# One layer with a chunked RWKV-7 recurrence: turning the triangular inverse with full transposes, and merging two state products

## The reference

```python
def step(s, inp):
    r_t, w_t, k_t, v_t, z_t, b_t = inp
    sz = jnp.einsum('bhvk,bhk->bhv', s, z_t)
    s = s * w_t[:, :, None, :] + sz[..., None] * b_t[:, :, None, :] + v_t[..., None] * k_t[:, :, None, :]
    return s, jnp.einsum('bhvk,bhk->bhv', s, r_t)
w = jnp.exp(-DECAY_SCALE * jax.nn.sigmoid(w0[d] + jnp.tanh(xw) @ w_lora[d]))
a = jax.nn.sigmoid(a0[d] + xa @ a_lora[d])
```

## Time and profile before

| | |
|---|---|
| median of 3 runs | 2143.8 us (2142.92 to 2143.82) |
| span of the profiled execution, first to last instruction | 2138.7 us |
| median less span | 5.1 us |
| TensorE busy, whole span | 2041.2 us (95%) |
| VectorE busy | 1196.4 us (56%) |
| ScalarE busy | 727.9 us (34%) |
| GpSimd busy | 234.2 us (11%) |
| recurrence, first X record to last | 594.5 to 863.4 us |

### The profile page before, as it was taken

One profiled execution on the slowest core, in us unless ns is written; L12 is line 12 of the kernel. 1 busy time (PEld: TensorE's weight loads), 2 busy tenths in 40 slices (PEclk: granted clock), 3 DMA queues, 4 the chain that ended last, 5 costly groups with the idle time before them and its releaser, 6 DMA issues.

```text
span 2138.7 us, 43718 instructions
## 1 busy us (share of the span) xinstructions
PE 2041.2 (95%) x18974; PEld 1810.3 (85%) x18974; DVE 1196.4 (56%) x2002; ACT 727.9 (34%) x1226; POOL 234.2 (11%) x381
## 2 busy tenths in 40 slices
PE   6999999998888889899999999999999999999997
PEld 3579999875677778687999999999999998887886
DVE  2347658865658786445655556546545544445544
ACT  3232222223554444233433233323333233333433
POOL 1001000002145454100000000000000000000001
PEclk9999999999989999999999999999999999999999
DMA  9998777664010100552644444444444446434341
GB/s 362 372 335 307 256 255 268 234 223 139 11 28 5 31 4 14 212 183 79 211 144 158 152 138 168 148 137 169 148 141 160 142 134 237 138 120 132 124 137 60
DMA packets 206064, 343.00 MB, mean 160 GB/s; under 512 B 15997, under 2 KB 139699, under 8 KB 203760
## 3 DMA queue, kind: packets, MB, share of 16 engines
q1 hardware_dynamic: 194560, 301.59, 41.3%
q0 software_dynamic: 11312, 38.61, 4.9%
HBM read 332.62 MB, written 10.31 MB: 160 GB/s over the span
## 4 chain that ended last, share of the span: by engine, by line
PE 86%; DVE 7%; DMA 3%; issue 2%; ACT 1%; POOL 1%; SPq 0%; DVEq 0%; ACTq 0%; POOLq 0%
PE ps L891 25%; PE ps L892 24%; PE ps L893 24%; DMA ring<-in_w_mod_dram 2%; PE ps L930 2%; PE ps L1143 1%; PE ps L1135 1%; PE ps L1153 1%; PE ps L1137 1%; PE ps L1262 1%; POOL w_mix L744 0%; PE ps L1226 0%; PE ps L1055 0%; PE ps L1069 0%; PE ps L1363 0%
## 5 line engine op out<-in xcount | busy, mean ns | idle before, releaser
L1823 DVE TENSOR_TENSOR w_split<-ring,w_split 128x1024 fp32r<-128x1024 f32 (+1 forms) x392 | 476.6, 1218 | 538.8 <-ACT w_split L1479 537.5
L1479 ACT ACTIVATE w_split<-ring 128x1024 fp32r<-128x1024 f32 (+1 forms) x392 | 411.4, 1052 | 842.4 <-PE ps L893 764.3
L891 PE MATMUL ps<-h_split,w_split 128*128 128x384 f32 x1776 | 595.9, 336 | 0.3 <-DVE h_split L2271 0.3
L893 PE MATMUL ps<-h_split,w_split 128*128 128x384 f32 x1776 | 593.4, 334 | 0.0
L892 PE MATMUL ps<-h_split,w_split 128*128 128x384 f32 x1776 | 593.4, 334 | 0.0
L891 PEld LDWEIGHTS ps<-h_split,w_split 128*128 128x128 f32 x1776 | 333.3, 188 | 7.9 <-issue 7.4
L892 PEld LDWEIGHTS ps<-h_split,w_split 128*128 128x128 f32 x1776 | 333.4, 188 | 0.0
L893 PEld LDWEIGHTS ps<-h_split,w_split 128*128 128x128 f32 x1776 | 333.3, 188 | 0.0
L891 PE MATMUL ps<-w_split,h_split 128*128 128x512 f32 (+1 forms) x528 | 200.5, 380 | 0.8 <-DVE w_split L1823 0.7
L893 PE MATMUL ps<-w_split,h_split 128*128 128x512 f32 (+1 forms) x528 | 196.4, 372 | 0.0
L892 PE MATMUL ps<-w_split,h_split 128*128 128x512 f32 (+1 forms) x528 | 196.4, 372 | 0.0
(11 more groups left out here) (392 smaller groups left out, 2669.2 us busy)
## 6 DMA issues: line engine op xcount, KB each, us to landing
ring<-in_w_up_dram SPq DMA_DIRECT2D x88, 1024.0 KB, 4.9
ring<-in_w_in_dram SPq DMA_DIRECT2D x46, 1024.0 KB, 7.2
ring<-in_w_down_dram SPq DMA_DIRECT2D x44, 1024.0 KB, 5.5
ring<-in_w_mod_dram SPq DMA_DIRECT2D x64, 512.0 KB, 7.5
ring<-in_w_mod_dram SPq DMA_DIRECT2D x32, 1024.0 KB, 6.2
arena<-in_w_mod_dram POOLq DMA_DIRECT2D x32, 512.0 KB, 5.2
ring<-in_w_out_dram SPq DMA_DIRECT2D x16, 1024.0 KB, 5.1
consts<-in_w_mod_dram POOLq DMA_DIRECT2D x64, 256.0 KB, 4.6
```

The source lines that it names most:

```text
L891: mm(o_, lh, rh, start=start, stop=False)
L893: return mm(o_, ll, rh, start=False, stop=stop)
L1479: AC(wh[k % SPLITS][:, 0:width(n)], arrived(n), ACT.Copy).then_inc(s_hi, 1)
L1823: V.tensor_tensor(wl[k % SPLITS][:, 0:w], arrived(n), wh[k % SPLITS][:, 0:w].bitcast(F32), ALU.subtract).then_inc(s_lo, 1)
```

## The change

- The turned inverse `TTm` is laid out head pair innermost: [p][hp][token][i] instead of [p][hp, i][token]. The masks, `T0i`, the T copy and GpSimd's `TTp` follow this layout, and T writes its PSUM columns two apart.
- X: instead of eight quadrant products with the identity, two transposes of 128x128 turn the inverse back, one for each i, ahead of the eight products with `Nm`. They write columns 128 to 383 of the bank. ScalarE now makes two copies, one into a new tile `XV` and one into a smaller `XT`, and T takes its stationary operand from `XV`.
- The state factor `Bbar` goes into the unused first matrix of `Am`, so that QMq gives the query weight and the state weight in one matmul of 128 columns; QMms keeps the two sums. GpSimd waits for the QMms of three units before ahead of it.
- lora: one matmul for both halves of the tokens, on 64 rows and all 128 columns, with a doubled identity `idc` for the bias.
- The cumulative sums (cum) stay on quadrants.

```diff
-                    for i in range(CT):
-                        for pair in (((0, 0), (1, 1)), ((1, 0), (0, 1))):
-                            for k in range(2):
-                                for c, hp in pair:
-                                    h = 2 * i + hp
-                                    o_ = halves(ps[half(hp), 4 * z + c, CHUNK * k + 32 * i:CHUNK * k + 32 * i + 32], l)
-                                    turned = TTm[z][half(c), slot(h), :]
-                                    if k == 0:
-                                        mm(o_, Nm[z][half(c), h, :], blocks(turned, l, 1 - d), start=True, stop=True)
-                                    else:
-                                        last = mm(o_, turned, blocks(ident[half(c), half(c)], l, d), start=True, stop=True)
+                    for i in range(CT):
+                        tr(ps[:, 4 * z, P * (i + 1):P * (i + 2)], TTm[z][:, :, :, i].rearrange("p a c -> p (a c)"), ident)
+                    for i in range(CT):
+                        for c, hp in ((0, 0), (1, 1), (1, 0), (0, 1)):
+                            h = 2 * i + hp
+                            last = mm(halves(ps[half(hp), 4 * z + c, 32 * i:32 * i + 32], l), Nm[z][half(c), h, :],
+                                      blocks(TTm[z][half(c), hp, :, i], l, 1 - d), start=True, stop=True)
...
-                            last = mm(halves(ps[half(c), 4 * z + hp, 32 * i:32 * i + 32], l), XT[z][half(hp), c, 1, HD * i:HD * i + HD],
-                                      blocks(XT[z][half(hp), c, 0, HD * i:HD * i + HD], l, d), start=True, stop=True)
+                            last = mm(halves(ps[half(c), 4 * z + hp, 0:CHUNK].rearrange("p (x i) -> p i x", i=CT)[:, i, :], l), XV[z][half(hp), i, c, :],
+                                      blocks(XT[z][half(hp), c, HD * i:HD * i + HD], l, d), start=True, stop=True)
...
-                            mm(ps[half(hp), 4 * z + c, HD * i:HD * i + HD], ZU[z][half(c), 2 * i + hp, 0, :], Am[v % 3][half(c), 2 * i + hp, 1, :],
-                               start=True, stop=True)
+                            mm(ps[half(hp), 4 * z + c, 0:2 * P].rearrange("p (m x) -> p m x", m=2)[:, :, HD * i:HD * i + HD],
+                               ZU[z][half(c), 2 * i + hp, 0, :], Am[v % 3][half(c), 2 * i + hp, 0:2, :], start=True, stop=True)
...
-                                        mm(ps[r, 4 * z + p, m_], ZU[z][c, h, 0, :], Bbar[z][c, hs], start=True, stop=True)
-                                    elif k == 1:
-                                        mm(ps[r, 4 * z + p, s_], Bbar[z][c, hs], ZU[z][c, h, 1, :], start=True, stop=False)
+                                        mm(ps[r, 4 * z + p, s_], Am[v % 3][c, h, 0, :], ZU[z][c, h, 1, :], start=True, stop=False)
...
-                    for c in range(2):
-                        for q, r in ((0, half(d)), (1, half(1 - d))):
-                            mm(ps[half(c), 2 + q, 0:HW], ident[r, r], par[pb][r, 2 * q + d, :], start=True, stop=False)
                     for q, r in ((0, half(d)), (1, half(1 - d))):
-                        for c in range(2):
-                            last = mm(ps[half(c), 2 + q, 0:HW], lora[r, q, P * t + CHUNK * c:P * t + CHUNK * (c + 1)], par[pb][r, 7 + q, :], start=False, stop=True)
+                        mm(ps[:, 2 + q, 0:HW], idc[r].rearrange("p c t -> p (c t)"), par[pb][r, 2 * q + d, :], start=True, stop=False)
+                    for q, r in ((0, half(d)), (1, half(1 - d))):
+                        last = mm(ps[:, 2 + q, 0:HW], lora[r, q, toks(t)], par[pb][r, 7 + q, :], start=False, stop=True)
...
-                    AC(XT[z].rearrange("p b k c -> p b (k c)").rearrange("p b (m s n) -> p b m s n", s=2, n=2 << l)[:, :, :, d, :],
-                       ps[:, 4 * z:4 * z + 2, 0:P].rearrange("p b (m n) -> p b m n", n=2 << l), ACT.Copy).then_inc(s_rXm, 1)
+                    AC(blocks(XV[z].rearrange("p i c t -> p (i c t)"), l, d), blocks(ps[:, 4 * z, P:3 * P], l, d), ACT.Copy)
+                    AC(XT[z].rearrange("p b (m s n) -> p b m s n", s=2, n=2 << l)[:, :, :, d, :],
+                       ps[:, 4 * z:4 * z + 2, 0:CHUNK].rearrange("p b (m n) -> p b m n", n=2 << l), ACT.Copy).then_inc(s_rXm, 1)
...
-                    V.copy_predicated(TTm[z].rearrange("p (a i) c -> p a i c", a=2), first_level,
-                                      ps[:, 2:4, :].rearrange("p a (i m c) -> p a i m c", i=CT, m=4)[:, :, :, 0, :]).then_inc(s_rT0, 1)
+                    V.copy_predicated(TTm[z], first_level, ps[:, 2:4, :].rearrange("p a (i m c) -> p a c i m", i=CT, m=4)[:, :, :, :, 0]).then_inc(s_rT0, 1)
...
-                    V.copy_predicated(TTm[z].rearrange("p h c -> p (h c)").rearrange("p (a m s n) -> p a m s n", a=2, s=2, n=n)[:, :, :, 1 - d, :], level,
+                    V.copy_predicated(TTm[z].rearrange("p a t i -> p a (t i)").rearrange("p a (m s n) -> p a m s n", s=2, n=n)[:, :, :, 1 - d, :], level,
...
-                    pool_tt(Bbar[z], btil[z], eT[z], ALU.mult)
+                    if v >= 3:
+                        pool.wait_ge(s_rQM, v - 2)
+                    pool_tt(Am[v % 3][:, :, 0, :], btil[z].rearrange("p (h c) -> p h c", h=HH), eT[z].rearrange("p (h c) -> p h c", h=HH), ALU.mult)
```

More of the change, by code:

```diff
@@ L257, in state_products @@
     return 2 * v + l + 1 - sum(UNITS[w % NG][0] == 0 for w in range(v + 1))
-def slot(h):
-    return (h % 2) * CT + h // 2
 def bank_of(m):
@@ L382, in build @@
         s2c, o = carve(wmix, o, 2, CHUNK)
-        idc, o = carve(wmix, o, CHUNK)
+        idc, o = carve(wmix, o, 2, CHUNK)
         par = [None, None]
@@ L392, in build @@
         assert o <= 2 * SPLITS * PART, o
-        Nm, XT, TTm, ZA, ZU, QT, zrT, bkT, MT, Sh, dP = ([None, None] for _ in range(11))
+        Nm, XT, XV, TTm, ZA, ZU, QT, zrT, bkT, MT, Sh, dP = ([None, None] for _ in range(12))
         ends = []
@@ L397, in build @@
             Nm[z], o = carve(region, 2 * PIECE if z == 0 else 0, HH, CHUNK)
-            XT[z], o = carve(region, o, 2, 2, P)
-            TTm[z], o = carve(region, o, HH, CHUNK)
+            XT[z], o = carve(region, o, 2, P)
+            XV[z], o = carve(region, o, CT, 2, CHUNK)
+            TTm[z], o = carve(region, o, 2, CHUNK, CT)
             ZA[z], o = carve(region, o, HH, 2, HD)
@@ L427, in build @@
         eE, eP, eT, kd, btil, ktil, tW, tA = ([carve(*early_out.pop(0), HW)[0] for z in range(2)] for _ in range(8))
-        Bbar, Kbar = eN, b1
+        Kbar = b1
         assert P_OUT // 2 % RING == 0 and N_SPLIT % SPLITS == 0
@@ L785, in _ @@
                     both = [blocks(xm[:, LEVELS * d + l, c, :], l, 1 - d).unsqueeze(1).broadcast_to([P, 2, 32 // (2 << l), 2 << l]) for c in range(2)]
-                    pool_tt(xmc[:, LEVELS * d + l, :].rearrange("p (i g n) -> p i g n", i=2, n=2 << l), *both, ALU.add)
-            pool_tt(idc, ident[:, 0:CHUNK], ident[:, CHUNK:P], ALU.add)
+                    pool_tt(xmc[:, LEVELS * d + l, :].rearrange("p (g n i) -> p i g n", i=CT, n=2 << l), *both, ALU.add)
+            for c in range(2):
+                pool_tt(idc[:, c, :], ident[:, 0:CHUNK], ident[:, CHUNK:P], ALU.add)
             pool_tt(s2c[:, 0], consts[:, C_SAME2:C_SAME2 + CHUNK], consts[:, C_SAME2 + CHUNK:C_SAME2 + P], ALU.add).then_inc(s_cc, 1)
@@ L792, in _ @@
             pool.wait_ge(s_cc, 2)
-            idb = idc.unsqueeze(1).broadcast_to([P, HH, CHUNK])
+            idb = idc[:, 0, :].unsqueeze(1).unsqueeze(3).broadcast_to([P, 2, CHUNK, CT])
             pool.wait_ge(s_grow, 1)
@@ L1152, in rwkv_step @@
                         for c in range(2):
-                            last = mm(ps[half(c), 4 * z, toks(h)], TTm[z][half(c), slot(h), :], ZA[z][half(c), h, :, :].rearrange("p a b -> p (a b)"),
+                            last = mm(ps[half(c), 4 * z, toks(h)], TTm[z][half(c), h % 2, :, h // 2], ZA[z][half(c), h, :, :].rearrange("p a b -> p (a b)"),
                                       start=True, stop=True)
@@ L1167, in rwkv_step @@
                         for pair in (((0, 0), (1, 1)), ((1, 0), (0, 1))):
-                            for k in range(3):
+                            for k in range(2):
                                 for p, hp in pair:
@@ L1171, in rwkv_step @@
                                     hs = slice(HD * h, HD * h + HD)
-                                    m_, s_ = (slice(q + HD * i, q + HD * i + HD) for q in (P, 2 * P))
+                                    s_ = slice(2 * P + HD * i, 2 * P + HD * i + HD)
                                     if k == 0:
-                                        mm(ps[r, 4 * z + p, m_], ZU[z][c, h, 0, :], Bbar[z][c, hs], start=True, stop=True)
-                                    elif k == 1:
-                                        mm(ps[r, 4 * z + p, s_], Bbar[z][c, hs], ZU[z][c, h, 1, :], start=True, stop=False)
+                                        mm(ps[r, 4 * z + p, s_], Am[v % 3][c, h, 0, :], ZU[z][c, h, 1, :], start=True, stop=False)
```

(8 more changed lines are left out.)

2 lines of the change are left out of this document (1 added, 1 removed).

## The result

| | before | after |
|---|---|---|
| median of six runs each | 2143.3 us (2139.23 to 2143.82) | 2149.57 us (2144.07 to 2150.73) |
| profiled execution, span | 2138.7 us | 2142.2 us |
| instructions | 43718 | 40425 |
| matmul records | 18974 | 17282 |

The ratio is 1.0033 [1.0021, 1.0044]: slower by 6 us, where the prediction had 13. The profiled execution of after took 2144.07 us, the fastest of its six, so spans are compared here only within the recurrence; its mean granted clock was 0.988, that of the other five 0.983 to 0.985.

A forecast was written before the change was run, and what follows sets the result against it. Neither TensorE nor VectorE was full; their hand-over in the recurrence was taken to bound it. TensorE's 18.1 + 3.6 - 1.6 = 20.1 us at 0.6, plus 0.9 from ScalarE, gave +13 us: 2156 us, range 2137 to 2171 (own range 2149 to 2165).

The forecast's parts named there:

- X step: TensorE, two transposes replacing identity products: +0.12 us at each of 90 levels, +0.12 more at 61 behind quadrants; 18.1 us.
- T step: TensorE's T product writing PSUM two apart: taken as no cost, upper bound 0.21 us a level, 19 us in all.
- Rival 3: Interleaved layout slows the T product (up to 0.21 us a level) or T0i: clearly slower, 2176 us; chance 0.10.
- ScalarE copy: X copy split in two: +0.05 us a level, mostly covered by other work; 0.9 us counted, 4.5 us uncovered.
- Low-rank step: TensorE, 8 quadrant matmuls become 4 of 64x128: +0.2 us a unit, 3.6 us; by the skill's rule +0.3, 5.4 us.
- QM: QMq and QMms on TensorE, state weight joined to the decay matrix: 1.06 instead of 1.15 us, -0.09 a unit, -1.6 us.
- VectorE: First level's copy into the inverse -0.15 us a unit, T0i up to +0.3; set against each other as 0.
- The share of 0.6: Part of added TensorE time taken to reach the end, from X products' 23.8 us on the chain against 39 us occupied.
- rival 1: Switches cost nothing at the transposes, fewer records, 2 us less "issue": faster, about -6 us, 2138 us; chance 0.17.
- The slack ahead of OL and S: TensorE idle 0.90 us while VectorE's QM is late, in half the units; only thing said to absorb later X products.
- ZU to ZU +0.7: Sign to check: one unit's ZU to the next's 0.7 us longer; if not, though steps fit, the 0.6 share is wrong.
- rival 2: VectorE sets the pace in units with F, a share of 0.2 remains: +4 us, 2144 to 2148; chance 0.15.

The follow-up runs named there:

- x_natural_order: Kernel before with only the X step changed, but the turned inverse kept in its old head order and VectorE's update in two instructions; 2148.49 us, 1.0029.
- before_copy_twice: Kernel before with ScalarE's copy of X in two instructions of 128 columns instead of one of 256; 2142.11 us, 1.0001.
- lora_only: Kernel before with only the low-rank step changed, 4 matmuls of 64x128 instead of 8 quadrant ones; 2141.37 us, 0.9993.
- qm_only: Kernel before with only the decay matrix and the state weight put into one product; 2138.55 us, 0.998.
- x_only: Kernel before with only the X step, its layout and copies changed; low-rank step, QMq and QMms as before; 2145.33 us, 1.0017.

## Why the prediction was right, point by point

- **X step: the mechanism right, the term somewhat too small.** "From rest +0.12" measured +0.20 (0.49 to 0.69), 0.07 of it the strided weight load, which the prediction didn't see, the rest 0.13. Where tr follows it has 0.80 instead of 0.61 to 0.63, and the switch in shows in the step ahead (ZU 0.92 to 1.02, AV 0.49 to 0.56, OL 0.47 to 0.56). ZU too loads the strided inverse, but in x_natural_order, where it is contiguous, ZU is 1.02 as well: it is the switch. The prediction took 0.49 us for all levels; level 0 had 0.75 and got only 0.05 longer. In the unit above, the five levels cost 0.05 + 0.20 + 0.25 + 0.17 + 0.20 = 0.87 us and ZU, OL and AV ahead 0.10 + 0.09 + 0.07 = 0.26, together 1.13, some 20 us for 18 units, where 18.1 stood. So the total came out nearer than its parts.
- **T step: right at nothing.** 0.20 us, T0i 436 ns. Rival 3 is out. The Trainium skill (Advanced Engine Details and Errata, Memory Cachelines) would have had T slow down and X not; the trace shows the opposite, T's write two apart costs nothing and the transposes' weight load two apart 0.07 us.
- **ScalarE copy: 0.9 us forecast, none found** (before_copy_twice).
- **Low-rank step: right on TensorE**, +0.19 for +0.2, but nothing on the time (lora_only). The Trainium skill (TensorEngine Tiling (Array Packing), Key Properties) has a change between quadrants and halves drain the array as well; by that the sum was +0.3. The trace gives +0.19 at the step, 0.05 more at QMq behind it (0.49 us, and 0.44 in qm_only, where no halves run ahead) and 0.11 more at X ahead of it (0.80 us, and 0.69 in x_only), 0.35 in all: it agrees with the page, and the 0.2 was too small. In lora_only the 0.11 is swallowed by the gap ahead of the step.
- **QM: the steps -0.01 instead of -0.09 a unit, the time -2.9 us instead of -1.6** (qm_only against its before). The steps did not get shorter, the pauses did.
- **VectorE: right.** 451 ns at most became 304, no loss at T0i, no effect on the time that any run shows.
- **The share of 0.6: wrong, and the largest error.** It took the X lines' part of the chain for the part of added work that would be paid. A unit is not uniform: what lies ahead of S is free in units with F steps (0.57 us added, nothing paid), what lies behind is paid but for the 0.37 us ahead of F2. Of the 0.57 + 0.90 us added to such a unit 0.51 were paid, a share of 0.35; in units without F steps nothing waits at S, and the period rose by 0.62 (14.21 to 14.83). "The slack ahead of OL and S" stood in the prediction as what is late next, but was given no number.
- **"issue": named only in rival 1, with 2 us.** The eight pauses of before were 9.3 us; their end takes back a part of the loss: with periods longer by 0.50 to 0.62 throughout, 17 intervals would be some 9 us longer, and they are 4.5. So about half of the pauses' 9.3 us was paid for, the rest fell into waits.
- **The sum.** +13 forecast: 20.1 x 0.6 + 0.9. Measured +6.3: some 9 us from X, low-rank and QM (0.51 x 18), less some 4 from pauses; the 1 to 2 us left over are not told apart from the spread of the runs. One at a time the three edits give +3.9, 0.0 and -2.9 us, +1.0 together; that the pauses can be taken away only once explains the 2.9, and the 2.4 us between x_only and after lie inside the intervals of the two. "ZU to ZU +0.7" was +0.51, which by the prediction's own sign says that the share of 0.6 was wrong. Rival 1 (switches free) and rival 2 (slack swallows all) each had a true half, the pauses and the first half of the unit. The direction was right by its mechanism; that 2149.6 us still lies in the forecast's own range, 2149 to 2165, at its very edge, is luck in part, since a share that was too large and pauses that were left out stand against switches that were priced too low.

## What to carry to other kernels

The share of a line on the chain is not the price of more work in that line. Cut the loop at the instruction where the engine waits for another, and ask for each added piece whether it lies ahead of the wait (free up to its length) or behind it (paid, unless a later wait takes it). An edit that takes small matmuls out may gain where no step gets shorter, in the pauses of the instruction stream: of the three edits here QM is the one to keep (2138.55 us) and the turned inverse the one to drop.

## What the runs showed of the hardware

- A dense stream of small matmuls pauses at some of the places that are 126.6 matmul records apart (253 with the weight loads), with distances of 0.8 to 2.7 us, 9.3 us in 285 us of before. It goes on 1.23 to 1.57 us after a 16 KB packet of the instruction queue has ended, in all 31 cases. With the 14 records a level fewer of x_only they were gone, with the 16 a unit fewer of qm_only they were 1.5 us, and a shift by 32 matmuls moved them to other steps.
- A 128x128 fp32 transpose whose stationary operand has its elements 8 bytes apart loads in 206 ns instead of 140, and a pair of them ends 0.07 us later. Matmuls that write 32 PSUM columns 8 bytes apart keep their 0.20 us.
- A change from quadrants into the full array costs 0.1 us (ZU 0.92 to 1.02) and the way back about 0.1 (0.20 us from the last transpose to the next quadrant product, where the next transpose comes in 0.11). Four matmuls on 64x128 between quadrants cost 0.35 us more than eight on 64x64 (0.11 ahead, 0.19 at the step, 0.05 behind).
- 32 unused fp32 matmuls of 2 columns to one quadrant take 5.7 us, 0.09 a record, most of it at a granted clock of 0.50, and delay the recurrence by 8.3 us.
